# Odd head's copy first on ScalarE, early first logits, low weight parts by GpSimd at two borders, rows interleaved by tile

## The reference

```python
for l in range(2):
    proj = einsum('bld,de->ble', h, w_in[l])
    a, g, zc, q, k, v, za, qi, ki, wi = split(proj, IN_SPLITS, axis=-1)
    y_conv = conformer_conv_branch(a, g, zc, ...)
    y_attn = dsa_sparse_attention(rope(q), rope(k), v, rope(qi), rope(ki), wi, topk) * silu(za)
    y = einsum('ble,ed->bld', concatenate([y_conv, y_attn]), w_out[l])
    h = layer_norm(ALPHA * h + y, post_ln_g[l], post_ln_b[l])
h = rmsnorm(x, norm_gain)
q, k, v, gate_a, u_in, v_in, gate_b, g_merge = split(einsum('bsd,de->bse', h, w_in), ...)
```

## Time and profile before

| | |
|---|---|
| median of 3 runs | 1060.81 us (1059.41 to 1061.35) |
| the profiled execution | 1061.86 us, span 1060.1 us |
| PE busy | 999.9 us, 94% |
| PEld busy | 845.2 us, 80% |
| DVE busy | 653.6 us, 62% |
| ACT busy | 582.7 us, 55% |
| POOL busy | 197.7 us, 19% |
| mean granted TensorE clock | 0.982 of full speed |

### The profile page before, as it was taken

One profiled execution on the slowest core, in us unless ns is written; L12 is line 12 of the kernel. 1 busy time (PEld: TensorE's weight loads), 2 busy tenths in 40 slices (PEclk: granted clock), 3 DMA queues, 4 the chain that ended last, 5 costly groups with the idle time before them and its releaser, 6 DMA issues.

```text
span 1060.1 us, 16512 instructions
## 1 busy us (share of the span) xinstructions
PE 999.9 (94%) x6452; PEld 845.2 (80%) x6452; DVE 653.6 (62%) x1423; ACT 582.7 (55%) x944; POOL 197.7 (19%) x238
## 2 busy tenths in 40 slices
PE   6999999898999899999999799789999899999997
PEld 6998988875577898898888577678888778887885
DVE  3899999866573489899977556626521433332522
ACT  6585882557444558587255734634555555554321
POOL 0000771013121100076101212223200000000001
PEclk9999999998999999999989999979999999999999
DMA  7776874734203777487464521765777545456651
GB/s 287 182 181 178 209 175 118 187 92 120 40 1 98 181 170 177 121 192 181 113 164 100 153 60 40 202 158 147 183 181 207 130 104 125 115 134 144 163 155 80
DMA packets 23820, 152.35 MB, mean 144 GB/s; under 512 B 2864, under 2 KB 3376, under 8 KB 6848
## 3 DMA queue, kind: packets, MB, share of 16 engines
q0 software_dynamic: 9648, 68.75, 34.8%
q1 hardware_dynamic: 14096, 82.55, 21.3%
HBM read 149.20 MB, written 2.10 MB: 143 GB/s over the span
## 4 chain that ended last, share of the span: by engine, by line
PE 61%; DVE 20%; ACT 9%; issue 7%; POOL 1%; DMA 1%; POOLq 0%; SPq 0%; DVEq 0%; ACTq 0%
PE psum_B L1246 15%; PE psum_A L1246 9%; PE psum_B L1279 7%; PE psum_A L1279 7%; DVE conv_acc L1723 6%; DVE score L1782 5%; PE psum_A L1428 5%; DVE top L1773 5%; PE psum_B L1428 2%; PE psum_A L1639 2%; PE psum_B L1382 2%; PE psum_B L1639 2%; ACT w_hi L631 2%; ACT w_lo L632 2%; PE psum_A L1357 1%
## 5 line engine op out<-in xcount | busy, mean ns | idle before, releaser
L1723 DVE SCALAR_TENSOR_TENSOR conv_acc<-u,vec,conv_acc 128x528 f32<-128x528 f32 (+1 forms) x240 | 172.1, 755 | 3.2
L1050 POOL DMA_DIRECT2D w_lo<-in_weights x67 | 59.4, 887 | 595.0 <-ACT w_lo L632 568.8
L1246 PE MATMUL psum_B<-x_hi,w_hi 128*128 128x264 f32 (+3 forms) x480 | 134.8, 321 | 5.2 <-DVE mlp_lo L2176 3.6
L631 ACT ACTIVATE w_hi<-w_raw 128x2048 fp32r<-128x2048 f32 (+2 forms) x85 | 129.3, 1521 | 15.0 <-DMA w_raw<-in_weights 14.5
L1246 PE MATMUL psum_B<-x_lo,w_hi 128*128 128x264 f32 (+3 forms) x480 | 132.5, 317 | 0.0
L1246 PE MATMUL psum_B<-x_hi,w_lo 128*128 128x264 f32 (+3 forms) x480 | 132.1, 316 | 0.0
L1246 PE MATMUL psum_A<-x_hi,w_hi 128*128 128x264 f32 (+2 forms) x528 | 127.3, 295 | 2.2 <-DVE za L1870 1.2
L632 ACT ACTIVATE w_lo<-w_raw 128x2048 fp32r<-128x2048 f32 (+2 forms) x85 | 128.6, 1513 | 0.0
L1246 PE MATMUL psum_A<-x_lo,w_hi 128*128 128x264 f32 (+2 forms) x528 | 124.6, 290 | 0.0
L1246 PE MATMUL psum_A<-x_hi,w_lo 128*128 128x264 f32 (+2 forms) x528 | 124.5, 290 | 0.0
L1246 PEld LDWEIGHTS psum_A<-x_hi,w_hi 128*128 128x128 f32 x528 | 89.4, 192 | 6.5 <-issue 3.3
(11 more groups left out here) (349 smaller groups left out, 2121.9 us busy)
## 6 DMA issues: line engine op xcount, KB each, us to landing
w_raw<-in_weights SPq DMA_DIRECT2D x67, 1024.0 KB, 5.2
w_lo<-in_weights POOLq DMA_DIRECT2D x65, 1024.0 KB, 8.4
x_first<-in_x_t SPq DMA_DIRECT2D x4, 528.0 KB, 6.9
h<-in_x SPq DMA_DIRECT2D x1, 2048.0 KB, 10.8
out<-h SPq DMA_DIRECT2D x4, 512.0 KB, 2.6
post_ln_g<-in_post_ln_g SPq DMA_DIRECT2D x2, 512.0 KB, 6.9
post_ln_b<-in_post_ln_b SPq DMA_DIRECT2D x2, 512.0 KB, 7.9
w_raw<-in_weights SPq DMA_DIRECT2D x2, 288.0 KB, 5.3
```

The source lines that it names most:

```text
L631: act.activation(whi[n % RING][:, a:b], raw[n % RING][:, a:b], ACT.Copy)
L1050: pool.dma_start(wlo[n % RING][:, 0:width], io["weights"][n, :, 0:width], accum_op=ALU.add) \
L1246: mm = pe.matmul(ps[0:cols, i, 0:b - a], w[wp][:, kt, at:at + cols], x[xp][:, kt, a:b], start=(kt == 0 and wp + xp == 0), stop=(kt == KD - ...
L1723: got = dve.scalar_tensor_tensor(dst, src, w, dst, ALU.mult, ALU.add)
```

## The change

The change has four parts.

1. **First logits.** TensorE issues the first pair's logits after the second early gate instead of the fourth. VectorE masks that pair after tap 90 (`TAPS_MASKED`), then does the two gates and the seven taps left. ScalarE's first two exponentials go ahead of the weight split.
2. **Odd head's copy.** `conv_affine` loses its tanh to a new `conv_tanh`. In each pair ScalarE first does what frees or holds banks for the even head (`bank_holders`: gate tanhs and affines), then the odd head's copy, then the rest of the woven work.
3. **Low parts by GpSimd.** For five blocks (`LO_BY_POOL`: a and g of layer 1, kv and both halves of q of the second block) ScalarE makes only the high part, in two halves of 128 x 1024, and GpSimd subtracts it from the raw block (`subtract_hi`), half by half. ScalarE's second copy and the adding transfer of these blocks go. The subtracts stand between GpSimd's deviations.
4. **Rows by tile.** The second block's rows come as kv 0, kv 1, q 0, kv 2, kv 3, q 1 to q 3 (`KV_AND_Q`), with the transpose of tile 3 behind kv 1 and that of tile 4 behind q 0. ScalarE's `x_hi` and `squares` of these tiles follow the rows. At the end of layer 1 the output half of tile 4 goes between the two halves of row (1, 3), and VectorE takes the residuals in that order; SP issues `load_mix` two blocks later.

The core of the diff (lines without a sign are context):

```diff
+KV_AND_Q = (("kv", 0), ("kv", 1), ("q", 0), ("kv", 2), ("kv", 3), ("q", 1), ("q", 2), ("q", 3))
...
+        uses.extend([(l, "wo", 0, 4, "conv"), (l, "wo", 1, 4, "conv"), (l, "wo", 1, 3, "conv")])
+        if l < DEPTH - 1:
+            uses.extend([(l, "wo", 1, 3), (l, "wo", 0, 4), (l, "wo", 1, 4)])
+        else:
+            uses.extend([(l, "wo", 0, 4), (l, "wo", 1, 3), (l, "wo", 1, 4)])
...
+    for half in range(2):
+        blocks.append(((l, "q", half), BLOCK, (l, "q", 3)))
+    uses.extend((l, *row) for row in KV_AND_Q)
...
+LO_BY_POOL = {NUMBER[key] for key in ((1, "a", 0), (1, "g", 0), (2, "kv", 0), (2, "q", 0), (2, "q", 1))}
...
+TAPS_MASKED = 90
...
-                if key == (2, "q", 1):
+                if key == (2, "vin", 0):
...
+                if n in LO_BY_POOL:
+                    for half in range(2):
+                        a, b = half * BLOCK // 2, (half + 1) * BLOCK // 2
+                        act.activation(whi[n % RING][:, a:b], raw[n % RING][:, a:b], ACT.Copy) \
+                            .then_inc(hi_made.mark(("w", n, half)), 1)
...
-                act.wait_ge(act_took.sem, act_took.at(use))
+
+            def conv_tanh(l, t):
+                n = SIZE[t]
+                act.wait_ge(act_took.sem, act_took.at((l, "back", t)))
...
+                exps(l, 0)
+                exps(l, 1)
...
+                        elif op[0] == "affine":
+                            conv_tanh(l, op[1])
+                        elif op[0] == "hi":
...
+                def bank_holders(i):
+                    for op in todo[i]:
+                        if op[0] in ("za", "zc"):
+                            gate_tanh(l, *op)
+                        elif op[0] == "affine":
+                            conv_affine(l, op[1])
+
                 for i in range(0, n, 2):
                     take_probs_t(l, i)
                     if i + 2 < n:
                         exps(l, i + 2)
                         exps(l, i + 3)
+                    bank_holders(i)
+                    take_probs_t(l, i + 1)
                     woven(i)
-                    take_probs_t(l, i + 1)
+                    bank_holders(i + 1)
                     woven(i + 1)
...
                     next_blocks((l, "wo", 1, 4))
                 else:
                     x_hi(l, 1)
+                    next_blocks((l, "wo", 0, 4))
                     x_hi(l, 2)
+                    next_blocks((l, "wo", 1, 3))
                     squares(3, square)
-                    next_blocks((l, "wo", 1, 3))
-                    x_hi(l, 3)
-                    squares(4, square)
-                    next_blocks((l, "wo", 1, 4))
-                    x_hi(l, 4)
 
 
...
-                for t in range(4):
-                    take_rows(name, t)
+            for name, t in KV_AND_Q:
+                take_rows(name, t)
+                if (name, t) == ("kv", 1):
+                    x_hi(DEPTH - 1, 3)
+                    squares(4, square)
+                elif (name, t) == ("q", 0):
+                    x_hi(DEPTH - 1, 4)
+                    split_hi(NUMBER[(2, "vin", 0)])
...
         def _(pool):
+            def subtract_hi(n, half):
+
+                a, b = half * BLOCK // 2, (half + 1) * BLOCK // 2
+                pool.wait_ge(hi_made.sem, hi_made.at(("w", n, half)))
+                pool.tensor_tensor(wlo[n % RING][:, a:b], raw[n % RING][:, a:b], whi[n % RING][:, a:b].bitcast(F32),
+                                   ALU.subtract).then_inc(pool_lo.mark((n, half)), 1)
...
-                next_blocks((l, "wo", 1, 4, "conv"))
-                ln_deviation((l, "post", 3), 3, P)
-                if l == DEPTH - 1:
+                if l < DEPTH - 1:
+                    a_in, g_in = NUMBER[(1, "a", 0)], NUMBER[(1, "g", 0)]
+                    subtract_hi(a_in, 0)
+                    subtract_hi(a_in, 1)
+                    ln_deviation((l, "post", 3), 3, P)
+                    subtract_hi(g_in, 0)
+                    subtract_hi(g_in, 1)
+                    ln_deviation((l, "post", 4), 4, P)
+                    next_blocks((l, "wo", 1, 4))
+                else:
+                    kv_in, q_in = NUMBER[(2, "kv", 0)], NUMBER[(2, "q", 0)]
+                    subtract_hi(kv_in, 0)
+                    subtract_hi(kv_in, 1)
+                    subtract_hi(q_in, 0)
+                    ln_deviation((l, "post", 3), 3, P)
+                    subtract_hi(q_in, 1)
                     input_deviation(3)
-                next_blocks((l, "wo", 1, 3))
-                ln_deviation((l, "post", 4), 4, P)
-                if l == DEPTH - 1:
+                    subtract_hi(q_in + 1, 0)
+                    ln_deviation((l, "post", 4), 4, P)
+                    subtract_hi(q_in + 1, 1)
...
+                elif n in LO_BY_POOL:
+                    pe.wait_ge(pool_lo.sem, pool_lo.at((n, 1)))
...
-                for gate, buf in zip(GATES_AHEAD, GATE_BANKS_AHEAD):
+                for j, (gate, buf) in enumerate(zip(GATES_AHEAD, GATE_BANKS_AHEAD)):
                     gate_half(l, *gate, buf)
+                    if j == 1:
+                        attention_logits(l, 0)
...
-                attention_logits(l, 0)
...
-                    turn_rows(l, 1)
-                output_rows(l, 1, 3, "A", 0)
                 if l < DEPTH - 1:
+                    output_rows(l, 1, 3, "A", 0)
                     turn_rows(l, 0)
                     turn_rows(l, 1)
-                output_attn(l, 0)
+                    output_attn(l, 0)
+                else:
+                    turn_rows(l, 1)
+                    ps = claim((l, "wo", 1, 3), "A", (0,))[:, 0, :]
+                    output_half(l, 1, 0, 3, ps).then_inc(psum_full.mark((l, "wo", 1, 3, "conv")), 1)
+                    output_attn(l, 0)
+                    output_half(l, 1, 1, 3, ps).then_inc(psum_full.mark((l, "wo", 1, 3)), 1)
...
 
-            for t in range(4):
-                x_ready(1, t + 1)
-                rows((2, "kv", t), NUMBER[(2, "kv", 0)], x, META + P * t, 1, 2 * P, 0, KD)
-                if t < 2:
-                    turn_rows(1, t + 3)
-            for t in range(4):
-                rows((2, "q", t), NUMBER[(2, "q", 0)], x, META + P * t, 2)
+            for name, t in KV_AND_Q:
+                if name == "kv":
+                    x_ready(1, t + 1)
+                    rows((2, "kv", t), NUMBER[(2, "kv", 0)], x, META + P * t, 1, 2 * P, 0, KD)
+                    if t == 1:
+                        turn_rows(1, 3)
+                else:
+                    rows((2, "q", t), NUMBER[(2, "q", 0)], x, META + P * t, 2)
+                    if t == 0:
+                        turn_rows(1, 4)
...
-                conv(l, 62, TAPS_AHEAD)
+                conv(l, 62, TAPS_MASKED)
...
+                masked_logits(l, 0)
+                masked_logits(l, 1)
                 for op in GATES_AHEAD[:2]:
                     gate(l, *op)
-                masked_logits(l, 0)
-                masked_logits(l, 1)
+                conv(l, TAPS_MASKED, TAPS_AHEAD)
...
+                    residual(l, 0, 4)
                     residual(l, 1, 3)
                     aggregate(l, 3)
                     post_norm(l, 3)
-                    residual(l, 0, 4)
                     x_lo(l, 2)
+                    residual(l, 1, 4)
                     second_input(3)
-                    residual(l, 1, 4)
```

29 lines of the change are left out of this document (10 added, 19 removed).

## The result

The changed kernel takes 1052.32 us (median of 4, 1051.08 to 1052.73) where the kernel before, run beside it, takes 1060.11 us: a ratio of 0.9927 with a 95% interval of 0.9907 to 0.9948. It is faster by 7.8 us, half of the 15.4 us forecast, and inside the stated range. The profiled execution took 1051.93 us.

What follows compares the result with a forecast made beforehand. TensorE, busy 94% of the span, was taken as the bound, with its waits and slow-clock stretches. Terms 6.5 + 6.3 - 3 + 6.1 - 0.5 = 15.4 us gave 1045.4 us on the median; range 1030 to 1055 us.

Steps and rivals of the forecast that it cites:

- First logits: Start of attention, layers 0 and 1: waits of 1.53 and 2.19 us and a slow-clock stretch go; 6.5 us gained.
- The 0.50 stretch from 529.50: Layer 1, slow clock beginning inside the 2.19 us wait for neg_max: expected gone with that wait, 3.2 us gained.
- Odd head's copies: Pairs of heads in attention: earlier second copies remove 5.9 us of waits and 2.4 of slow clock, less 2: 6.3 gained.
- the give-back: Attention: tanh and y come about 0.5 us later, with conv work, deviation and transposes back behind them; 2 us lost.
- half: Attention's slow-clock stretches from 246.20 and 587.50 cost 4.75 us; half was taken as saved by the copies, 2.4 us.
- Border of layers 0 and 1: GpSimd's subtracts hold VectorE's norm passes, wait for x_lo becomes about 5.7 us, g's wait goes; 3 us lost.
- Border of layer 1 and block 2: The seven pieces up to the second q row take 28.3 us instead of 34.4; 6.1 us gained.
- The 1.7 us for tile 3: Border of layer 1 and block 2: h_normed of tile 3 comes 1.7 us late.
- vin: Second block's split after the second q row: its accumulating transfer has about 1 us of room; 0.5 us lost.
- no exclusion that matters: Rival at both borders: VectorE slips in between the subtract halves; 31.3 us gained in all, 1029.5 us; chance 0.2.
- The bound moves in attention: Rival: other waits replace the copies', clock stays at 0.50; attention gives 5 us, 7.6 in all, 1053.2 us; chance 0.17.
- slower, by the port: Rival: more passes wait for subtracts; borders lose 5.6 and 0.6 us, attention gives 4; 2.7 lost, 1063.5 us; chance 0.05.

Runs made afterwards that it cites:

- the attention parts alone: Only the hunks for first logits and odd head's copies, borders as before, against the kernel before: 1049.02 us, ratio 0.9894.
- the borders alone: All hunks but those of attention (low parts by GpSimd and interleaved rows), against the kernel before: 1062.79 us, ratio 1.0015.

## Why the prediction was half right

**First logits, 6.5 us forecast, 3.3 measured alone.** The 3.7 us of waits went, and VectorE's taps came back without harm. The step that failed is "The 0.50 stretch from 529.50 begins inside the 2.19 us wait, so I expect it gone too: half of its 6.36 busy us, 3.2 us". With the copies alone that wait stands at 2.17 us and no stretch follows, and with the first logits alone the stretch went in the trace but the median gained only the waits. A wait that a stretch follows in one trace is not shown to be its cause.

**Odd head's copies, 6.3 forecast, 7.2 measured alone.** Waits of 7.0 us went where 5.9 were counted, and 2.5 us came where 2 were given back. Only the growth at the conv norm (0.70 to 1.25 us) stands where the give-back put it; most of the rest is waits for copies and affines, and the 1.46 us at the affines come from the split ahead of them in ScalarE's queue. The stretches came out otherwise than "half": that of layer 0 stayed, that of layer 1 grew from 3.40 to 8.31 busy us, and those at 270 and 529.5 went. Which part saves which stretch is left open: the ten runs of the first logits alone lie 6 us apart, and one profile shows one of them. For the two parts together 11.2 us were measured (7.6 to 15 by the interval) against 12.8, and some of that is luck: in the trace of the attention parts 3.3 us of it fall at a border that the forecast left out of them.

**Border of layers 0 and 1, 3 us lost forecast.** The subtract came 0.15 us ahead of the pass, where 0.1 was forecast. Passes of over 3 us beside subtracts of 2.4, a wait of 5.08 us where 5.7 was worked out, and a stretch at 0.50 behind it: 5.08 - 1.05 - 2.40 and half of 3.80 busy us make 3.5 us lost by the trace, and 1.9 by putting the transfers back. The mechanism is settled by moving g's subtracts.

**Border of layer 1 and block 2, 6.1 gained forecast, 8.4 by the trace** (34.4 less 26.0). The 3.3 us at the second kv row were 3.56, the 1.8 at tile 4 were 1.70. The 1.7 us for tile 3 and the 1.0 for q's second half did not come. The second kv row ran at 0.50, which may have covered them; no run tests it. Of the 8.4 us up to 3.3 are not this part's own, since the attention parts alone shortened the border by as much in one trace. The range for a half subtract, 1.3 to 3.2 us, held 2.4; twice the median of the short one, 2.55, was near.

**vin, 0.5 us lost forecast, 6.8 measured.** This is the step that halved the gain: "its accumulating transfer has about 1 us of room before the row needs it". The prediction gives no time for the load that comes first. With the usual 5.1 us (the page's median) the block would have come 5.0 us earlier, 1.1 us ahead of its use: the room that was forecast. kv's last row is now one q row nearer to vin, and the load, issued at 692.8, met the adding transfer of vin's first block and landed after 10.1 us; split and transfer took it 3.9 us past its use, and a stretch at 0.50 cost half of 5.09 us more: 6.4 us. That the transfer beside it makes the load slow was not tested. In three traces with this order, the change's and those of the borders alone and of vin by GpSimd, the two ran together and took 10.1 to 10.4 us and 10.6 to 10.9 us.

**The sum.** Attention gave 11.2 us, the borders 8.4 - 3.5 - 6.8 = -1.9 us: 9.3, or down to 6.0 where the 3.3 us at the border are counted once; 7.8 were measured. The kernel with the borders alone (1.6 us lost) agrees with the -1.9. Of the rivals, "no exclusion that matters" is refuted by g's move. "The bound moves in attention" is the one whose total, 7.6 us, lies nearest to the 7.8 measured, but that is chance: its price for attention was 5 us and 11.2 were measured, though a third of the copies' waits did move on as it said. The time lies inside the range because the range was drawn for that rival; the loss at vin was in no rival. The price of "slower, by the port" (5.6 and 0.6 us lost at the borders) was reached at neither.

**What beats both kernels.** The change with vin's second block by GpSimd and the subtracts of g and q on VectorE, and x_lo of tile 2 ahead of tile 4's residual: 1039.05 us, ratio 0.9805 (0.9773 to 0.9836) to the kernel before.

## What to carry to other kernels

Before work goes to GpSimd, look at what VectorE does in the same microseconds: a subtract of 2.4 us there held VectorE for 1 to 2 us each time that a two-input pass stood beside it, while VectorE's own took 1.2 us and fitted into its waits. When rows are reordered, follow every buffer that comes free later, to the end of the chain behind it (load, split, transfer), with the loads' times as they are beside other transfers (10.1 us here instead of 5.1). Book the saving of a slow-clock stretch as a chance, not as a term: which wait it follows changed from kernel to kernel.

## What was not expected of the hardware

Exclusion did not stop at instructions with two SBUF tensors. Beside GpSimd's subtract a normalisation of 128x400, one tensor and a scalar per row, took 2.33 us instead of 0.43. The Trainium skill (SBUF — State Buffer, section "Who interferes with whom") counts tensor_scalar, under conditions on its operands, among the forms that can take the ports shared with GpSimd. This trace agrees (2.33 us instead of 0.43), and the prediction had counted two-input passes only.

It works against GpSimd too. The first step of a deviation, on 128 numbers, took 0.19 us at 337.74 and 1.28 us at 346.50, just behind the start of a norm pass, in the kernel with g's subtracts on VectorE:

```profile
337.74 0.19 POOL L1103 TENSOR_SCALAR var_eps<-meanvar 128x1 f32<-128x1 f32 x1 [0.87 <-DVE meanvar L1989]
...
346.50 1.28 POOL L1103 TENSOR_SCALAR var_eps<-meanvar 128x1 f32<-128x1 f32 x1 [7.95 <-DVE meanvar L1989]
...
346.45 1.29 DVE L1999 SCALAR_TENSOR_TENSOR h<-h,meanvar,post_ln_g 128x1024 f32<-128x1024 f32 x1
...
348.53 1.28 DVE L2003 SCALAR_TENSOR_TENSOR h<-h,rstd,post_ln_b 128x1024 f32<-128x1024 f32 x1 [0.79 <-POOL rstd L1106]
```

The kernel before shows the same: seven such steps issued just behind the start of a pass of 1.28 us took 1.27 or 1.28 us, four behind the start of a pass of 0.75 us took 0.75. So a deviation issued beside a pass comes about 1.1 us later, and the second pass here waits 0.79 us for it.
